# Three of four second MLP products as two groups of seven products, with sums of weight quarters formed in HBM, and six raw weight tiles in place of ten

## The reference

```python
xn = rms_norm(x, g_mix)
u, q, k, v, gates = split(xn @ w_in)            # 1024 -> 512 + 3*512 + 2*1024
y_pool = trailing means of u (windows 2, 4, 8, 16) minus u, one 128x128 map per group, a scale
y_sb   = stick-breaking attention of q, k, v    # 8 heads of 64, strictly causal
x = x + (gate_a * (y_pool @ w_pool_up) + gate_b * (y_sb @ w_sb_up)) @ w_out
x = x + square(relu(rms_norm(x, g_mlp) @ w_up)) @ w_down          # 1024 -> 4096 -> 1024
x = x + sigmoid(rms_norm(x, g_ple) @ w_ple_gate) * (p @ w_ple_proj)
y = rms_norm(x, g_final)
```

## Time and profile before

| | |
|---|---|
| median of 3 runs | 788.3 us (787.94 to 789.0) |
| the profiled execution | 788.06 us, span of its instructions 786.3 us, 1.76 us around it |
| PE busy | 771.5 us, 98% of the span |
| DVE, ACT, POOL busy | 496.7, 389.9, 97.1 us |
| granted TensorE clock | 0.995 |
| DMA | 110.19 MB, of it 20.97 MB in 40 adding DMAs and 84.72 MB on SP's queue |

### The profile page before, as it was taken

The page is one execution under the profiler, slowest core; times in us unless marked ns, Lnnn a source line. Parts: engine busy times, 40 slices in busy tenths (PEclk is TensorE's granted clock), DMA queues, the critical chain, the costliest instruction groups (busy, mean ns, idle before and its releaser), DMA issues.

```text
span 786.3 us, 14379 instructions
## 1 busy us (share of the span) xinstructions
PE 771.5 (98%) x6046; PEld 764.0 (97%) x6046; DVE 496.7 (63%) x615; ACT 389.9 (50%) x464; POOL 97.1 (12%) x171
## 2 busy tenths in 40 slices
PE   9999999999999999999999999999999999999994
PEld 9999999999999899999999999999999999999993
DVE  6776556556665637787763367424763357677986
ACT  7545525525675442765641255214642145556566
POOL 1040230240240000020001100010001100100001
PEclk9999999999999999999999999999999999999998
DMA  7241322222222217786566846586475856825503
GB/s 239 98 146 57 103 86 63 100 80 71 93 82 62 100 54 215 241 204 172 182 170 169 201 164 186 145 206 167 158 212 127 208 175 172 217 70 136 160 1 114
DMA packets 34250, 110.19 MB, mean 140 GB/s; under 512 B 4624, under 2 KB 6672, under 8 KB 34192
## 3 DMA queue, kind: packets, MB, share of 16 engines
q1 hardware_dynamic: 25920, 84.72, 33.4%
q0 software_dynamic: 6016, 21.04, 14.8%
q10 hardware_dynamic: 2256, 3.60, 1.3%
HBM read 94.33 MB, written 4.52 MB: 126 GB/s over the span
## 4 chain that ended last, share of the span: by engine, by line
PE 91%; DVE 4%; ACT 3%; issue 1%; POOL 0%; POOLq 0%; DVEq 0%
PE psum L1458 22%; PE psum L1157 20%; PE psum L1163 20%; PE psum L1160 20%; PE psum L1206 1%; PE psum L1337 1%; PE psum L1234 1%; PE psum L1232 1%; PE psum L1194 1%; PE psum L1193 1%; ACT xt L1077 1%; ACT w_hi L737 1%; PE psum L1213 1%; PE psum L1218 1%; ACT L763 0%
## 5 line engine op out<-in xcount | busy, mean ns | idle before, releaser
L737 ACT ACTIVATE w_hi<-raw_more 128x1024 fp32r<-128x1024 f32 x84 | 88.7, 1057 | 133.0 <-PE psum L1163 100.6
L1160 PE MATMUL psum<-b_lo,w_hi 128*128 128x272 f32 x688 | 142.0, 288 | 0.0
L1157 PE MATMUL psum<-b_hi,w_hi 128*128 128x272 f32 x672 | 139.3, 289 | 0.0
L1163 PE MATMUL psum<-b_hi,w_lo 128*128 128x272 f32 x672 | 138.9, 288 | 0.0
L1590 DVE TENSOR_TENSOR w_lo<-raw_more,w_hi 128x1024 fp32r<-128x1024 f32 x84 | 102.2, 1223 | 34.5 <-ACT w_hi L737 34.3
L1157 PE MATMUL psum<-a_hi,w_hi 128*128 128x272 f32 x576 | 120.6, 291 | 0.5 <-DVE w_lo L1582 0.5
L1163 PE MATMUL psum<-a_hi,w_lo 128*128 128x272 f32 x576 | 119.2, 288 | 0.0
L1160 PE MATMUL psum<-a_lo,w_hi 128*128 128x272 f32 x576 | 118.8, 288 | 0.0
L1458 PE MATMUL psum<-u_hi,w_hi 128*128 128x272 f32 x560 | 116.1, 289 | 0.2 <-ACT h_of L981 0.2
L1458 PE MATMUL psum<-u_hi,w_lo 128*128 128x272 f32 x560 | 115.7, 288 | 0.0
L1458 PE MATMUL psum<-u_lo,w_hi 128*128 128x272 f32 x560 | 115.5, 287 | 0.0
(11 more groups left out here) (263 smaller groups left out, 1015.4 us busy)
## 6 DMA issues: line engine op xcount, KB each, us to landing
raw_more<-w_tiles SPq DMA_DIRECT2D x84, 512.0 KB, 4.3
raw<-w_tiles SPq DMA_DIRECT2D x66, 512.0 KB, 3.5
raw_more<-w_tiles POOLq DMA_DIRECT2D x16, 512.0 KB, 6.8
raw_more<-raw_more POOLq DMA_DIRECT2D x14, 512.0 KB, 8.4
xt<-x_t SPq DMA_DIRECT2D x8, 272.0 KB, 5.6
y_t<-xt SPq DMA_DIRECT2D x16, 136.0 KB, 1.9
raw<-w_tiles POOLq DMA_DIRECT2D x4, 512.0 KB, 7.7
raw_more<-raw POOLq DMA_DIRECT2D x3, 512.0 KB, 6.7
```

The costliest lines, as they stand in the source:

```text
L737: act.activation(w_hi[:, t % W_RING, :, :].rearrange("p k c -> p (k c)"), src, ACT.Copy)\
L1157: pe.matmul(base[:, h, :], w_hi[:, s, wk, :], at(hi, k, h * HALF, (h + 1) * HALF), start=(opens and q == 0), stop=False, skip_group_check= ...
L1160: pe.matmul(base[:, h, :], w_hi[:, s, wk, :], at(lo, k, h * HALF, (h + 1) * HALF), start=False, stop=False, skip_group_check=True)
L1163: mm = pe.matmul(base[:, h, :], w_lo[:, s, wk, :], at(hi, k, h * HALF, (h + 1) * HALF), start=False, stop=(closes and q == len(ks) - 1), s ...
```

## The change

For the first three chunks (`SEVENS`) the second product takes the Winograd form too. The 1024 input features of a chunk are the two groups of hidden features, and the 1024 outputs are two halves (e = 0, 1). Each of the seven products of a half runs over both groups, so there are 14 weight tiles `("dn", c, s, e)` of 24 matmuls in place of 8 of 48; the two halves take turns. The last chunk keeps the plain `down`.

The activations need sums for this as well: per group of hidden features DVE forms four (NT1, T3, NT2, T4) from the squared quarters, ACT and DVE split seven operands into hi and lo, 544 elements per partition each, in place of two operands of 1088. Fourteen results per chunk are added to or subtracted from quarters of `xt` (`second_taken`), in place of eight.

The sums of the second product's weights are not made in the raw buffers. POOL issues 24 copies and 24 adding DMAs from HBM to HBM into `sums_t`, in steps behind the masks of the attention heads, and before each step waits for all DMAs of the step before (`sums_behind`). The `dn` loads then take one finished tile each. The 32 sums of the first products stay as they were, but POOL issues them group by group (S1, S2, S4, S3), not mixed over the two groups of a chunk. The raw buffers are six, since `t_more`, with seven more operands of 544, takes the room.

```diff
-T_CHUNK = 2 * T_UP + KT
+T_CHUNK = 4 * T_UP
-RAW_BUFS = 10
+RAW_BUFS = 6
+SUM_STEPS = ((("S1", "A21"), ("S3", "A21"), ("S2", "A11"), ("S4", "A12")), (("S1", "A22"), ("S3", "A11")),
+             (("S2", "S1"),), (("S4", "S2"),))
...
+    sums_t = nc.dram_tensor("sums_t", (len(SUMS) * DN_GROUPS, P, KT * P + SUM_PAD), F32, kind="Internal").ap()
...
+                elif name[0] == "dn" and SIDES[name[2]] in SUMS:
+                    g = 2 * name[1] + name[3]
+                    sp.wait_ge(sums_in, sums_made(g, len(SUM_STEPS) - 1))
+                    sp.dma_start(raw_buf(n), sums_t[len(SUMS) * g + SUMS.index(SIDES[name[2]]), :, :])\
+                        .then_inc(raw_in[raw_at(n)], 16)
...
+            def sum_step(g, step):
+                for what, of in SUM_STEPS[step]:
+                    if step == 0:
+                        pool.dma_start(sum_tile(g, what), sum_tile(g, of)).then_inc(sums_in, 16)
+                    else:
+                        pool.dma_start(sum_tile(g, what), sum_tile(g, of), accum_op=ALU.add).then_inc(sums_in, 16)
+
+            def sums_behind(k):
+                if 0 < k:
+                    pool.wait_ge(sums_in, sums_made(k - 1, 0))
+                for g in range(max(0, k - len(SUM_STEPS) + 1), min(k + 1, DN_GROUPS)):
+                    sum_step(g, k - g)
+
             for g in range(HEADS):
...
                 pool.wait_ge(prob_done, g + 1)
                 mask_diagonals(pm_done)
+                sums_behind(g)
                 if g % 2 == 0 and g != HEADS - 2:
                     window_mean(g // 2, sums)
...
             for c in range(CHUNKS):
-                for g, what in ((0, "S1"), (0, "S2"), (1, "S1"), (0, "S4"), (0, "S3"), (1, "S2"), (1, "S3"), (1, "S4")):
-                    second_part(2 * c + g, what)
+                for g in range(2):
+                    for what in ("S1", "S2", "S4", "S3"):
+                        second_part(2 * c + g, what)
...
+            def up_seven(g):                                # ACT
+                for s in range(T_UP):
+                    n = NTH[("up", g, s)]
+                    if s == 0 and g % 2 == 1:
+                        last_quarter_hi(g - 1)
+                        sum_hi(g - 1, "NT1")
+                    ahead(t_up(g, s))
+                    if s == 0 and g % 2 == 1:
+                        sum_hi(g - 1, "T3")
...
+                    if g and s == 0:
+                        act.wait_ge(olo_done, nth_lo(g - 1, "NT1"))
+                        act.wait_ge(sum_done, nth_t(g - 1, "NT2"))
+                    if g and s == 1:
+                        if g % 2 == 1:
+                            sum_hi(g - 1, "T4")
+                        act.wait_ge(olo_done, nth_lo(g - 1, "NT2"))
+                        act.wait_ge(sum_done, nth_t(g - 1, "T4"))
...
+                    if BY_ACT[s]:
+                        copy_quarter(g, n, s)
...
+            def down_seven(c):                              # PE
+                for from_group in range(2):
+                    for e in range(2):
+                        if from_group == 0:
+                            weights(t_dn(c, 0, e))
+                            place_for(NTH[("dn", c, 0, e)])
+                        if e == 0:
+                            pe.wait_ge(olo_done, nth_lo(2 * c + from_group, "B11"))
+                        mm = second_product(c, 0, e, from_group)
...
+            def second_taken(c, s, e):                      # DVE
+                n, side = NTH[("dn", c, s, e)], SIDES[s]
+                x = x_quarter(side, e)
...
+                dve.wait_ge(full, n + 1)
+                dve.tensor_tensor(x, x, slot(n), ALU.subtract if X_QUARTER[side][0] else ALU.add).then_inc(taken, 1)
```

More of the change, by code:

```diff
@@ L39 @@
 T_UP = 7
[L40 to L41 removed]
+SEVENS = CHUNKS - 1
+T_CHUNK = 4 * T_UP
+T_PLE = T_MLP + SEVENS * T_CHUNK + 2 * T_UP + KT
 N_TILES = T_PLE + 2 * (T_UP + 1)
@@ L143, in staged_loads @@
             seq.extend((g, what) for what in LOADS)
-        seq.extend(("down", c, q) for q in range(KT))
+        if c < SEVENS:
+            seq.extend(("dn", c, s, e) for s in range(T_UP) for e in range(2))
+        else:
+            seq.extend(("down", c, q) for q in range(KT))
     seq.extend((UP_GROUPS, what) for what in LOADS)
@@ L536, in source, with sums_made @@
             return raw_buf(n), (raw_in[raw_at(n)], raw_count(n))
+        def sums_made(g, step):
+            return 16 * sum(len(SUM_STEPS[k - h]) for k in range(g + step + 1)
+                            for h in range(max(0, k - len(SUM_STEPS) + 1), min(k + 1, DN_GROUPS)))
         block = ctx.enter_context(nc.Block())
@@ new lines, in operand_sum @@
+            def operand_sum(g, name):
+                first, second = {"NT1": ("B11", "B12"), "T3": ("B22", "B12"), "NT2": ("B22", "NT1"),
+                                 "T4": ("NT2", "B21")}[name]
+                over = {"NT1": "B11", "NT2": "B22", "T4": "B21"}.get(name)
+                if over:
+                    dve.wait_ge(olo_done, nth_lo(g, over))
+                if name == "NT1":
+                    dve.wait_ge(ohi_done, nth_hi(g, "sq B12"))
+                if name != "NT1":
+                    dve.wait_ge(sum_done, nth_t(g, T_ORDER[T_ORDER.index(name) - 1]))
+                if name in ("NT1", "T3"):
+                    ins = dve.tensor_tensor(hidden(name), hidden(first), hidden(second), ALU.subtract)
+                else:
+                    ins = dve.scalar_tensor_tensor(out=hidden(name), in0=hidden(first), scalar=-1.0,
+                                                   in1=hidden(second), op0=ALU.mult, op1=ALU.subtract)
+                ins.then_inc(sum_done, 1)
@@ L2210 @@
             tiles += group_tiles(part, group_starts(g))
-        tiles += column_tiles(w_down[0, D_MODEL * c:D_MODEL * (c + 1)], ordered)
+        part = w_down[0, D_MODEL * c:D_MODEL * (c + 1)]
+        if c < SEVENS:
+            for g in range(2):
+                tiles += group_tiles(part, group_starts(g))
+        else:
+            tiles += column_tiles(part, ordered)
     for g in range(2):
```

266 lines of the change are left out of this document (222 added, 44 removed).

## The result

The changed kernel takes 805.98 us (median of 4 runs), the kernel before 788.23 in the same call: a ratio of 1.0237, 95% interval 1.0221 to 1.0253. It is slower, as forecast, but by 17.8 us and not by 2.8: 791 was 15 us too low. The time lies outside the likeliest case (784 to 799), in the span given to rival B (799 to 815), and inside the whole range (777 to 808). The profiled execution took 804.64 us.

The account below looks back on a forecast made before the run. PE bounds the kernel, if its weights arrive in time: 788.06 - 17.9 (matmuls) + 5.7 (first groups) + 10.0 (second groups) + 2.5 (DVE) + 2.6 (gate) = 790.96, so 791 us; 8-in-10 range 777 to 808.

Parts of the forecast that it names:

- likeliest case: Forecast that the changed kernel's time lies between 784 and 799 us, chance 0.55.
- rival B: Congestion: each MLP addition but a second group's first takes 8.0 us, giving 813 us; span 799 to 815, chance 0.13.
- What goes: In the second products of three chunks PE loses 144 matmuls, saving 17.9 us.
- Second groups: In chunks 1 to 3 result 1's copy is late behind S3's split: stalls 2.8, 2.8 and 4.4, together 10.0 us.
- First groups: In chunks 1 to 3 result 1's copy is late behind S3's split: 1.9 us each, 5.7 us together.
- an addition of 6 us or less: Sign of being wrong: the adds of the first groups land in 6 us or less.
- DVE: DVE's burst costs 1.0 us in chunk 0 and 0.5 at each entry into `dn`, 2.5 us together.
- Gate: In the gate's second group S4' lands late, so split, square and copy stall PE by 2.6 us.
- the granted clock: Sign of being wrong: idle PE lets the granted clock fall below 1.00; no time was added for it.
- Attention: POOL's HBM copies and additions beside attention were taken to cost nothing, its masks keeping their distances.
- Rival C: Attention is held by slow HBM copies and additions, 10 us late in each of three full steps: 821 us, chance 0.05.
- Rival A: The chain of additions is quick and the kernel gets faster: 774.2 us if all quick; span 774 to 784, chance 0.25.

Follow-up runs that it names:

- run without chains: Changed kernel with sums of groups 3, 5 and 7 also made in HBM, and the gate's S2' and S4' added by POOL: 777.81 us, 0.9898.
- attention's part alone: Kernel before plus the 24 copies and 24 additions in HBM beside attention, results unused: 790.28 us, 1.0031.
- POOL's own sums: Changed kernel with S2 and S4 of the first products computed by POOL in all groups, in place of adding DMAs: 787.86 us, 1.0001.
- the third sum cut: Changed kernel with the adding DMA of S3 in the MLP moving 16 of 1024 columns: 801.68 us, 1.0183.
- POOL for S4' alone: Changed kernel with only S4 of the second groups computed by POOL, S2 staying an adding DMA: 809.06 us, 1.027.
- POOL in second groups only: Changed kernel with S2 and S4 computed by POOL in second groups only, first groups keeping their adding DMAs: 795.13 us, 1.0102.
- The single run with 48: Kernel before plus unused HBM sums for one group in place of six, 4 copies and 4 additions: 789.14 us.

## Why the prediction came out as it did

- **What goes**: 144 matmuls, 17.9 us. Right: 5902 instructions, and 754.6 us of PE work where the clock is whole (771.5 - 17.9 = 753.6).
- **Second groups**, 10.0 forecast, 12.8 measured. The chain was right: the load of S1' held until S4 lands, then load and three additions, 26.0 us where I had 22.9 in chunk 1. There it was the middle addition, 7.9 for 6.0, and the first, 7.0 for 5.7; in chunk 3 the first took 9.6. The place was not right: PE waits for result 0 behind S4' and not for result 1 behind S3'. I had set only the later path against its time. By my own terms the earlier one was late as well: S4' at P'+6.1, split 1.06, 0.66 and 0.62 give P'+8.4 against 5.97, a stall of 2.5 that falls into the same 2.8. The run without chains shows chain and additions to be the cause, and that with another order of loads adds what I had left out: the hand-over is not by itself the bound, since an earlier load lands later beside the additions.
- **First groups**, 5.7 forecast, 1.05 measured. Mis-sized: S4 lands at P + 2.8 in chunk 1 and not at P + 5.9. Its S1 was added at P - 17.0 (I had P - 15.7) and took 5.8, not the 7.8 of the earlier trace rows. I had named an addition of 6 us or less as a sign that I am wrong. The four errors on waits (-4.65, +2.8, -1.5 and +3.25, the last two below) cancel to 0.1 us: that the waits came to 20.7 for 20.8 is luck.
- **DVE**, 2.5 forecast, 1.0 measured, in chunk 0. Entering `dn` costs nothing. In the run without chains the burst itself lets PE wait nowhere in chunks 1 to 3.
- **Gate**, 2.6 forecast, 5.85 measured, and by another way: the addition of S2' took 10.7 us, with the DMA engines at 1.05 of their time, and it held ACT's split, DVE's low part and behind them the embedding's result, whose slot PE wanted. Rival B's duration, at one place.
- **What was left out: the granted clock.** I had it among the signs of error, with no price. Behind each of the four long stalls PE ran for a stretch at 1.2 GHz: 11.0 us of busy time over the sum, 10.0 by the comparison with equal instructions, 10.6 by the windows. This is the largest part of the 15 us of error. No row of before showed it, so a bound was wanted: matmuls at half the clock for as long as PE had stood, and that belonged in the upper end of the sum. That the range held the time was the margin left for slow additions, and not this.
- **Also left out: the end.** 2.0 us behind the last matmul. The HBM DMAs brought them in the run of attention's part alone, but the 9.4 us of the run with POOL's own sums show that they are not a fixed price of those DMAs.
- **Attention**: nothing, right. Rival C is out even with 72 such DMAs: PE is busy for 298.8 of 300 us from 40 to 340 us, as before, at 0.77 of the DMA engines' time.

The sum with what was measured: 786.3 - 17.9 + 1.05 + 12.8 + 1.0 + 5.85 + 10.0 + 2.0 = 801.1 against a span of 802.9. Of the 1.8 left, 0.5 is idle PE at 56 us, 1.0 the rest of the 11.0 of busy time (not explained further); 0.3 stays open. The same parts, each less its forecast (-4.65, 2.8, -1.5, 3.25, 10.0, 2.0, 1.8), make the 13.7 us between 790.96 and the profiled 804.64. Rival B's 813 was nearer than my forecast, but not for its reason: the median addition took 6.9 us, not 8.0. Rival A fell with the chain.

## What to carry to other kernels

Count buffers in time, not in tiles: when a change halves the work per tile, the same number of buffers reaches half as far ahead. A chain of dependent DMAs that hid behind ten buffers cost some microseconds with six, and four to five per second group once the tiles were halved too. Set each result that is copied behind the chain against its own due time; the first that is late is where the engine stops. Price a TensorE stall twice, once for its length and once for the slow stretch behind it: four stalls of 3.95 to 5.85 us (18.6 together) cost 10.0 us more. When a chain is late, take it out of the stage and make its results where the queues are idle, rather than start it sooner or hand it to an engine that shares something with the one behind it.

## What the runs showed of the hardware that was not expected

- TensorE's clock: up to the gate, idle times of 1.0 to 2.1 us left it at 2.4 GHz in every run. Behind the four of 3.95 to 5.85 us in the changed kernel it stood at 1.2 GHz for some 6.8 us each, whatever the length, part of that still in the stall. For idle times in between, in other runs, the stretch is 3.4 us (1.7 us of clock missing, behind 2.35 us with the third sum cut, 3.34, 3.51 and 3.97 us) or 6.8 (behind 3.00 us in the run with POOL for S4' alone), and the length of the idle time doesn't say which; 2.38 us in the run with both groups by POOL left the clock whole.
- POOL adds 128x1024 of fp32 in 2.8 us on the mean, not in the 2.1 that 573 columns in 1.16 us suggest. It holds up DVE's operations with both inputs in SBUF, and not those with one in PSUM.
- A copy of 512 KB from HBM to HBM took 14.2 us in the median, up to eight of them and of the additions in flight, and PE was busy for 298.3 of 300 us beside them, 298.8 before.
- The end of the program, from PE's last matmul on, grows with the DMAs that POOL issues into HBM and SBUF together. It is 9.0 us with the 40 of the kernel before, 9.4 with 68 (both groups by POOL), 10.1 with 78 (POOL in second groups only), 11.0 with the changed kernel's 88 and 11.7 with 98 (no chain in the second groups). The single run with 48 is out of line, at 9.7.
